# Moving the activations of both up projections by 16 and 48 bytes in SBUF

## The reference

```
# block 1                                    # block 2
z = h @ w_up            # 2048 x 11264       gate = h @ w_gate      # 2048 x 5632
z = causal 3-tap convolution of z            val  = h @ w_up        # 2048 x 5632
gate, val = split(z)                         y = (silu(gate) * val) @ w_down
y = (gelu(gate) * val) @ w_down
```

## Time and profile before

| | |
|---|---|
| time, median of 3 runs | 3183.25 us (3182.97, 3183.25, 3200.63) |
| the profiled execution's own time | 3179.22 us |
| its span, first to last instruction | 3177.4 us |
| PE busy | 3016.8 us, 95% |
| DVE, ACT, POOL busy | 1804.6, 1272.2, 321.1 us |
| first up projection | 788.3 to 1282.8 us |
| second up projection | 2442.3 to 2923.9 us |
| mean granted TensorE clock | 0.97 of 2.4 GHz |

### The profile page before, as it was taken

How to read it: one execution, slowest core, us unless ns; L and a number is a source line. 1 busy time by engine, 2 the same in 40 slices (tenths; PEclk the granted TensorE clock), 3 DMA queues, 4 the chain that set the end, 5 groups by cost and what they waited for, 6 DMA issues and landing times.

```text
span 3177.4 us, 43194 instructions
## 1 busy us (share of the span) xinstructions
PE 3016.8 (95%) x18045; PEld 2606.3 (82%) x18045; DVE 1804.6 (57%) x1704; ACT 1272.2 (40%) x1155; POOL 321.1 (10%) x460
## 2 busy tenths in 40 slices
PE   8899999996999999999698999989998999999998
PEld 3588777875999999888587888867877999999886
DVE  1376777787677776544545446754544444444444
ACT  0134544433444444344333333434433444444433
POOL 1000000001000000000105816620000000000000
PEclk9999999997999999999798999999998999999999
DMA  9777777893666655655345652226643555555564
GB/s 356 277 281 260 286 284 274 305 386 137 249 242 225 236 199 187 226 211 201 133 170 180 220 184 77 84 73 217 244 160 132 197 188 197 191 192 211 201 213 168
DMA packets 110499, 671.55 MB, mean 211 GB/s; under 512 B 23521, under 2 KB 25697, under 8 KB 33313
## 3 DMA queue, kind: packets, MB, share of 16 engines
q1 hardware_dynamic: 101584, 626.96, 54.7%
q0 software_dynamic: 8800, 42.97, 3.6%
HBM read 652.48 MB, written 17.40 MB: 211 GB/s over the span
## 4 chain that ended last, share of the span: by engine, by line
PE 89%; DVE 5%; DMA 3%; ACT 1%; issue 1%; SPq 0%; POOL 0%; DVEq 0%; POOLq 0%; ACTq 0%
PE acc L1800 27%; PE acc L1801 26%; PE acc L1802 26%; PE ms L1870 3%; PE tp L1845 2%; DVE w_lo L1130 1%; DMA w_raw<-ada_stream 1%; DMA w_raw<-w_stream 1%; DVE mod_sum L1205 1%; PE ms L2235 1%; PE acc L2264 0%; PE acc L2274 0%; DVE y L1171 0%; DMA ada<-ada_stream 0%; PE ms L2234 0%
## 5 line engine op out<-in xcount | busy, mean ns | idle before, releaser
L1130 DVE TENSOR_TENSOR w_lo<-w_raw,w_hi 128x2048 fp32r<-128x2048 f32 x484 | 1111.6, 2304 | 850.3 <-ACT w_hi L755 831.4
L755 ACT ACTIVATE w_hi<-w_raw 128x2048 fp32r<-128x2048 f32 x484 | 923.5, 1915 | 1071.3 <-DMA w_raw<-w_stream 1069.6
L1800 PE MATMUL acc<-h2T_hi,w_lo 128*128 128x256 f32 x2816 | 785.0, 279 | 3.5 <-DVE h2T_lo L1144 3.5
L1801 PE MATMUL acc<-h2T_lo,w_hi 128*128 128x256 f32 x2816 | 784.5, 279 | 0.0
L1802 PE MATMUL acc<-h2T_hi,w_hi 128*128 128x256 f32 x2816 | 784.4, 279 | 0.0
L1800 PEld LDWEIGHTS acc<-h2T_hi,w_lo 128*128 128x128 f32 x2816 | 530.3, 188 | 4.0 <-issue 4.0
L1801 PEld LDWEIGHTS acc<-h2T_lo,w_hi 128*128 128x128 f32 x2816 | 532.5, 189 | 0.0
L1802 PEld LDWEIGHTS acc<-h2T_hi,w_hi 128*128 128x128 f32 x2816 | 531.9, 189 | 0.0
L1800 PE MATMUL acc<-w_hi,hid_lo 128*128 128x512 f32 x704 | 275.1, 391 | 4.5 <-DVE w_lo L1130 4.5
L1801 PE MATMUL acc<-w_lo,hid_hi 128*128 128x512 f32 x704 | 274.8, 390 | 0.0
L1802 PE MATMUL acc<-w_hi,hid_hi 128*128 128x512 f32 x704 | 274.7, 390 | 0.0
(11 more groups left out here) (503 smaller groups left out, 3968.9 us busy)
## 6 DMA issues: line engine op xcount, KB each, us to landing
w_raw<-w_stream SPq DMA_DIRECT2D x484, 1024.0 KB, 4.8
ada<-ada_stream SPq DMA_DIRECT2D x64, 1024.0 KB, 6.9
w_raw<-ada_stream SPq DMA_DIRECT2D x32, 1024.0 KB, 4.8
g_dram<-gates_out SPq DMA_DIRECT2D x12, 512.0 KB, 7.0
gates_in<-g_dram POOLq DMA_DIRECT2D x12, 512.0 KB, 5.9
bias_rows<-b_in POOLq DMA_DIRECT2D x18, 256.0 KB, 6.2
x_res<-x POOLq DMA_DIRECT2D x2, 2048.0 KB, 13.6
g_dram<-gate_stage SPq DMA_DIRECT2D x8, 512.0 KB, 6.0
```

What stands on the lines that cost most here:

```text
L755: sc.activation(whi[:, s % 4], raw[:, s % 4], ACT.Copy).then_inc(hi_made, 1)
L1130: v.tensor_tensor(wlo[:, s % 4], raw[:, s % 4], whi[:, s % 4].bitcast(F32), ALU.subtract).then_inc(lo_made, 1)
L1800: mm(o, sl, mh, start=start, stop=False, skip_group_check=share)
L1801: mm(o, sh, ml, start=False, stop=False, skip_group_check=share)
```

## The change

`h2T` now starts 16 bytes higher than before, at 48 bytes below a multiple of 256, and serves the first up projection alone. The second gets tiles of its own name, `h3T`, at 112 bytes below. Both are cut out of a slightly larger allocation by `shifted`. The tiles still lie in the same 32 KB, the instructions of each engine and their order are the same, and so are the values.

```diff
+        def shifted(name, kb, off):
+            t = u(name, [P, KD * S + 64], kb, F32R)
+            return t[:, off // 4:off // 4 + KD * S].rearrange("p (k s) -> p k s", s=S)
...
-        h2T = [u("h2T_hi", [P, KD, S], -B64, F32R), u("h2T_lo", [P, KD, S], 16 - B64, F32R)]
+        h2T = [shifted("h2T_hi", -B64, 16), shifted("h2T_lo", 16 - B64, 16)]
+        h3T = [shifted("h3T_hi", -2 * B64, 16), shifted("h3T_lo", 16 - 2 * B64, 16)]
...
             squares(lambda k: x[:, k], lambda k: m2[:, k], P, (0, 1)).then_inc(sem("ssq"), 1)
-            turns_hi(h2T[0], KD)
+            turns_hi(h3T[0], KD)
...
             dve.sem_inc(sem("m2"), 1)
-            turns_lo(h2T, KD)
+            turns_lo(h3T, KD)
...
             def up():
                 with engine_loop(pe, FC // 2, (m, 8), (chunks, 2)) as i:
                     for _ in range(2):
-                        cols_chunk(h2T)
+                        cols_chunk(h3T)
```

## The result

| | before | after |
|---|---|---|
| median of 5 runs each, us | 3183.25 | 3216.68 |
| profiled execution's own time, us | 3179.22 | 3216.69 |
| its span, us | 3177.4 | 3214.9 |

The ratio after to before is 1.009, with a 95% interval of 1.0054 to 1.0126. The change makes the kernel slower by about 0.9%, clear of the runs' uncertainty, where I had forecast a small gain within 1%.

What follows compares the result with a forecast made beforehand. PE was taken as the bound, matmul count times pace. Saving 12 us in the first up projection and none in the second turned the 3183.3 us median into 3171 us, range 3135 to 3227.

Steps and rivals of the forecast that it cites:

- the sum passes 32 us: Up projections: mean pace from which a slowdown would exceed 1% of the kernel, put at 118.8 ns.
- The writers: 16 ACT and 16 DVE instructions writing the tiles to shifted addresses: costed at nothing, 2 us at most.
- Two lasting patterns: First up projection at 64 below: small disturbances switch PE's operand and weight streams between 113.3 and 117.8 ns per matmul.
- Inside these bounds I take 113.3 ns for both: Both up projections at their new addresses: 113.3 ns chosen, saving 12 us in the first, nothing in the second.
- the slow pattern: First up projection, 919 to 1239 us: 2,688 matmuls at 117.8 ns instead of 113.3, expected to vanish, saving 12 us.
- The floor: Moving stream in both up projections: 113.3 ns taken as best pace, 1/16 above one column per period.
- the streams meet worse: Rival, both up projections: shifted rows keep colliding with weight loads; 120.0 ns, 44 us more, 3227 us; chance 0.23.
- The first rival: Both up projections: streams meet better than in any row; at 110 ns 40 us less, 3143 us; chance 0.28.
- The fourth: Rival: address indifferent below 64 bytes; 3183 us, second projection open from 113.3 to 120.0 ns; 0.21 including patterns dealt anew.
- The bounds: Pace at the new addresses in both up projections: 106.7 ns (68 us less) to 120.0 ns (44 us more).
- the likeliest case: Both up projections at 113.3 ns throughout: 12 us less, 3171 us, own range 3160 to 3180; chance 0.28.
- The rule on two read ports: Weight loading takes no read bandwidth from the running matmul, so addresses would not matter: zero effect, 3183 us.

Runs made afterwards that it cites:

- e1: Changed kernel with the second up projection's tiles back at 64 bytes below, the first's still at 48 below; 3192.1 us, ratio 1.0029 to before.
- e2: Changed kernel with the first up projection's tiles back at 64 bytes below, the second's still at 112 below; 3202.8 us, ratio 1.0052 to before.
- e5: Kernel before with five one-column matmuls instead of four in each group between pairs of chunks; 3192.0 us, ratio 1.0025.
- e6: Kernel before with six one-column matmuls instead of four in each group between pairs of chunks; 3193.9 us, ratio 1.0035.
- the small kernel: Separate kernel, computing nothing of the reference, streaming PE matmul blocks at varied operand addresses while ACT, DVE and DMA idle; 113.3 to 120.0 ns in up-projection blocks 16 bytes apart.
- The map: Paces of up-projection-like matmul blocks, run alone, with activations 0 to 240 bytes below a multiple of 256: 113.3 to 120.0 ns; further shapes were added later.
- The widths: Blocks run alone with moving operands of other column counts: 111.7 ns from 128 to 224 columns, 146.7 for 320, 173.3 at best for 384.

## Why the prediction was wrong, point by point

- **What bounds the kernel, and the arithmetic.** Right. PE is the bound in both projections, the time is count times pace, 4.2 us per nanosecond and projection; 119.2 and 118.7 ns give 12.9 and 22.8 us by it, and the trace has 12.6 and 21.2 (before's second projection had lost more at its start, with a granted clock of 0.50 over 6 us against 0.72 after). Two slips in the sums changed no conclusion: the sum passes 32 us from a mean pace of 118.5 ns on, not 118.8, and at 109.2 ns both projections would save 47 us, not 51, which counts the 3.9 us of small work as saved.
- **The writers cost nothing.** Right: 0.60 and 0.69 us as before.
- **Two lasting patterns, switched by small disturbances.** Right: in before, e1, e2, e5 and e6 the pace changes at groups of one-column matmuls or at the transpose and nowhere else inside a projection, and the small kernel shows both paces at one address. What decides which of the two follows is open.
- **The step that failed** is "Inside these bounds I take 113.3 ns for both". I said there that it was a choice and not a reading, and it was the wrong way round. Its reason was that every stretch outside the slow pattern ran at 113.3, but these stretches were all at one distance, 64 below. The only other distance of this shape in the rows was at 120.0. One fast and one slow address are no ground for giving the fast pace to two new ones. The map shows how things lie: of 16 distances in steps of 16, two reach 113.3 and the median is 118.3. The rows of `nT`, whose starts go round the multiples of 64, already said that an average address is slow: 126.1 ns for 272 columns. That it gives 118.7 when scaled, as measured at 112 below, is luck: the map has 123.3 at best for 272 columns, not the 120.4 that scaling from 256 would give. What the step cost: forecast 12 us saved in the first projection and none in the second, measured 12.6 and 21.2 us lost.
- **The floor.** The number held, no distance was under 113.3 ns, but not its reason. I read 113.3 for 256 and 226.7 for 512 columns as one pace per column, 1/16 above the period. The widths show 13.3 ns above the columns' own time at 320, 384 and 512 columns alike, and 6.7 at 256. And the earlier trace rows, 16 stationary columns at 113.3, didn't show a floor of the moving stream: with 16 columns 64 and 112 below are slower.
- **The rivals.** What happened is the second, "the streams meet worse", with 0.23. Its price, 120.0 ns and 44 us, was near: 119.2 and 118.7 ns, 33.8 us in the two projections. Its picture, a row that covers 17 pieces of 64 bytes, is refuted: 144 below covers 17 as well and is the fastest, and 0, 128 and 192 cover 16 and are slow. The first rival (a better meeting than in any row) has no address in the map. The fourth (no difference under 64 bytes) falls with 48 below, 119.2 ns where 64 below has 113.3 or 117.8; 112 and 128 below, 118.7 and 118.6 in the map, would have agreed with it.
- **The bounds.** 120.0 was not the upper end: 123.3 at 252 below. The range of 3135 to 3227 still held the time, but by way of a rival and not by the forecast: the likeliest case's own range ended at 3180, and the kernel moved by 33 us the other way.
- **The rule on two read ports** (the Trainium skill, page "TensorE: Matmul & The Clock Gate", part 2, step 1) I had weighed and set aside. The runs show by how much the address matters with nothing else running: 113.3 to 123.3 ns for the same instructions. They don't show whether ports, banks or something else in the read path is shared.

What stays open: the rule behind the map. It repeats after 256 bytes of distance, depends on the weights' own start (tried at 144 below, where it repeats after 32 bytes), on the width of the moving operand and of the load, and on what ran just before. I have no model that gives the paces from these, and don't offer one.

## What to carry to other kernels

Where a loop is bound by PE and its moving operand takes about as long to stream as the next weights take to load, the start address of the moving tile within 256 bytes was worth up to 9% of the loop in the small kernel (113.3 to 123.3 ns) and 6% in whole kernels (113.3 to 120.0), and it couldn't be reasoned out from one or two addresses: measure the candidates in a small kernel with the same shapes. Here it gave the whole kernels' paces to a tenth of a nanosecond, with one exception: e1's 116.7 ns at 48 below, a second pace that it never showed. Take each behind several leads and choose one that is fast behind all of them (144 below, -0.6% on the kernel), not one that is fast behind some (64 below); that makes a slow pattern less likely and doesn't exclude it. Do it again for another width: 0 below was the best for 512 columns and among the worst for 256.

## What was not expected of the hardware

- Identical matmuls at one address pair ran for hundreds of microseconds at 113.3 or at 117.8 ns, and the switch from one to the other came at a single transpose or a group of one-column matmuls.
- The pace changes from one 4-byte step to the next (113.3 at 144 below, 121.7 at 140, 120.0 at 148), and moving weights and activations together from a multiple of 256 by 16 bytes moves it too (120.0 to 116.7), by 64 not.
- 128 to 224 moving columns all ran at 111.7 ns per matmul beside 128x128 loads; 320, 384 and 512 at best at 13.3 ns above one column per period of 2.4 GHz.
